# A diffusion trunk layer on eight cores: attention masks added on TensorE, normalizing passes on GpSimd, and a new order of projections and attention

## The reference

```
h    = modulate(layer_norm(x), shift, scale)             # adaLN from SiLU(c) @ w_ada
q, k, v, u, vb, ga, gb = split(h @ w_in)
ya   = attention(rope(q), rope(k), v)                    # band of +-128 tokens, plus 256 context keys,
                                                         # plus a sink logit; 8 query, 2 key heads
yb   = gelu(u) * (W_s @ layer_norm(gelu(vb)) + b_s)      # per chunk of 128 tokens
mix  = (sigmoid(ga) * (ya @ w_a) + sigmoid(gb) * (yb @ w_b)) @ w_out
xm   = layer_norm(alpha * x + gate1 * mix)
out  = layer_norm(alpha * xm + gate2 * swiglu(modulate(layer_norm(xm))))
```

## Time and profile before

| | us |
|---|---|
| median of 3 runs | 969.98 (969.21 to 974.94) |
| the profiled execution | 974.86 |
| its slowest core (core 6), first to last instruction | 973.1 |
| its quickest core (core 5) | 966.4 |
| PE busy on core 6 | 890.9 (92%) |
| DVE, ACT, POOL busy | 622.9, 317.7, 284.6 |

### The profile page before, as it was taken

One profiled execution on the slowest core, in us unless ns is written; L12 is line 12 of the kernel. 1 busy time (PEld: TensorE's weight loads), 2 busy tenths in 40 slices (PEclk: granted clock), 3 DMA queues, 4 the chain that ended last, 5 costly groups with the idle time before them and its releaser, 6 DMA issues.

```text
span 973.1 us, 15750 instructions; the slowest of 8 cores (966.4 to 973.1 us)
## 1 busy us (share of the span) xinstructions
PE 890.9 (92%) x5495; PEld 446.2 (46%) x5589; DVE 622.9 (64%) x1131; ACT 317.7 (33%) x494; POOL 284.6 (29%) x231
## 2 busy tenths in 40 slices
PE   1389688898999999999999999999999999999995
PEld 1235444344554444444444544444444444444673
DVE  4337686857655666766687476556656674666787
ACT  1436775546867243334435200111111001011110
POOL 6024263555554233324312540202202021111111
PEclk9999898979999999999999999999999999999999
DMA  8997622339963500026321480303213020111112
GB/s 203 202 187 190 174 87 66 88 46 161 164 95 81 174 1 1 1 88 100 114 47 44 173 192 25 87 1 87 36 52 87 0 44 1 44 44 57 52 66 87
DMA packets 30380, 83.91 MB, mean 86 GB/s; under 512 B 2912, under 2 KB 3168, under 8 KB 28640
## 3 DMA queue, kind: packets, MB, share of 16 engines
q0 software_dynamic: 18064, 34.54, 22.9%
q1 hardware_dynamic: 12240, 48.37, 14.2%
HBM read 109.05 MB, written 8.39 MB: 121 GB/s over the span
## 4 chain that ended last, share of the span: by engine, by line
PE 84%; DMA 6%; DVE 4%; issue 3%; ACT 2%; POOL 1%; DVEq 0%; POOLq 0%; SPq 0%; ACTq 0%
PE psum L1178 31%; PE psum L1204 15%; PE psum L1016 11%; PE psum L1033 6%; PE psum L1067 6%; DMA arena<-wqk 4%; PE psum L673 3%; PE psum L729 3%; PE psum L900 2%; PE psum L936 2%; PE psum L760 2%; DMA arena<-ctxb 1%; DVE arena L495 1%; PE psum L1102 1%; DVE arena L974 1%
## 5 line engine op out<-in xcount | busy, mean ns | idle before, releaser
L1178 PE MATMUL psum<-arena 128*128 128x512 bf16 (+1 forms) x1515 | 314.5, 361 | 1.1
L1178 PEld LDWEIGHTS psum<-arena 128*128 128x128 bf16 x1536 | 150.2, 98 | 154.5
L1184 ACT ACTIVATE arena<-psum 128x512 f32<-128x512 f32 (+1 forms) x96 | 53.9, 562 | 380.4 <-PE psum L1178 380.4
L1204 PE MATMUL psum<-arena 128*128 128x512 bf16 x681 | 161.0, 379 | 1.9 <-DVE arena L1187 0.7
L508 POOL TENSOR_TENSOR arena<-arena 128x1 f32<-128x1 f32 (+1 forms) x74 | 70.9, 958 | 287.2 <-DVE arena L506 272.0
L1218 DVE TENSOR_TENSOR arena<-arena,psum 128x512 f32<-128x512 f32 x224 | 140.5, 679 | 18.8 <-PE psum L1204 18.6
L1187 DVE TENSOR_TENSOR arena<-psum,arena 128x512 bf16<-128x512 f32 (+1 forms) x96 | 62.0, 646 | 131.2 <-PE psum L1178 127.8
L1016 PE MATMUL psum<-arena 128*128 128x512 bf16 x498 | 115.7, 379 | 1.4 <-issue 1.0
L495 DVE BATCH_NORM_STATS2 arena<-arena 128x6 f32<-128x512 f32 x152 | 99.7, 685 | 14.5 <-DMA arena<-xh 3.8
L1204 PEld LDWEIGHTS psum<-arena 128*128 128x128 bf16 x704 | 68.6, 98 | 82.7 <-issue 2.6
L906 ACT ACTIVATE arena<-psum 128x1024 bf16<-128x1024 f32 (+1 forms) x100 | 80.7, 852 | 23.2 <-PE psum L900 22.1
(11 more groups left out here) (95 smaller groups left out, 883.2 us busy)
## 6 DMA issues: line engine op xcount, KB each, us to landing
arena<-xh SPq DMA_DIRECT2D x34, 512.0 KB, 7.7
arena<-wada POOLq DMA_DIRECT2D x24, 512.0 KB, 18.0
arena<-wff POOLq DMA_DIRECT2D x11, 1024.0 KB, 9.2
arena<-wff SPq DMA_DIRECT2D x11, 1024.0 KB, 7.0
out<-arena SPq DMA_DIRECT2D x15, 512.0 KB, 2.6
arena<-wc POOLq DMA_DIRECT2D x8, 768.0 KB, 20.0
arena<-wout SPq DMA_DIRECT2D x8, 512.0 KB, 4.4
arena<-rope SPq DMA_DIRECT2D x4, 512.0 KB, 11.5
```

Source lines behind the costliest of these rows:

```text
L1178: ins = e.matmul(bank(ps)[:, 0:n], lhsT=w1v[r][:, k, lo:lo + 128], rhs=h2(k), start=(k == 0), stop=(k == 7))
L1184: s = P.op('act', prio - 150, act_cost(n), lambda e: e.activation(out=sgv(), in_=bank(pg)[:, 0:n], func=AF.Silu), after=[a], takes=[sg], g ...
L1204: ins = e.matmul(bank(ps), lhsT=actv[(r, fi, t)], rhs=w2v[r][:, fi, h * 512:(h + 1) * 512], start=(n == 0), stop=(n == 2 * len(rounds) - 1))
```

## The change

- **Masks.** For tiles 0 to 3 the product on POOL (line 915) goes. In its place a matrix `shut` (0 where a key counts, about -1e30 where not) is made once on DVE, and one more matmul per score block adds it through the identity to the scores in PSUM before the exponential: 4 tiles x 2 blocks x 2 key heads = 16 matmuls of 128x512. Tiles 4 to 15 keep the product.
- **Norm passes.** Groups 2 and 3 normalize their tiles on DVE and POOL in turn instead of all on ACT, the group `hal` on DVE and ACT instead of all on ACT. In `proj_v`, odd tiles do the scaling on POOL (`ZPOOL`), straight from mean and rstd, in place of line 525 on DVE and line 774 on ACT.
- **Loads.** The table `rope 0` waits for piece 5 of `wada`, and with it SP's queue. Group 2's x waits for `wu1` instead of `wu3`. Group 3's first two x tiles get two buffers of their own. The gate pieces 8 to 11 of `wada` wait for the second x tile of group 3 (`ld_x3[1]`) instead of `wvvb`.
- **Order.** The planner's `LAG` of POOL goes from 0.12 to 1.2, some durations rise a little, and nearly every priority of the projections, the spatial mixing and the attention is another number.

```diff
-    LAG = {'pe': 0.24, 'act': 0.10, 'dve': 0.10, 'pool': 0.12, 'sp': 0.1}
+    LAG = {'pe': 0.24, 'act': 0.10, 'dve': 0.10, 'pool': 1.2, 'sp': 0.1}
...
-    rope_load('0', 14, rope_d[0], 512, [])
+    rope_load('0', 14, rope_d[0], 512, [ada_ld[5]])
...
-    norm_group('2', [xh[(9 + i) * 128:(10 + i) * 128, :] for i in range(4)], 29, [ld_wu[3]])
-    norm_group('hal', [xh[0:128, :], xh[17 * 128:18 * 128, :], ctxb[0:128, :], ctxb[128:256, :]], 30, [ld_wu[3]])
+    norm_group('2', [xh[(9 + i) * 128:(10 + i) * 128, :] for i in range(4)], 47.5, [ld_wu[1]], ('dve', 'pool'))
+    norm_group('hal', [xh[0:128, :], xh[17 * 128:18 * 128, :], ctxb[0:128, :], ctxb[128:256, :]], 20.1, [ld_wu[3]], ('dve', 'act'))
...
-            r, st = stat(prio + i, [gvs], 512, [[ge]], EPS)
-            mi = minus(st, prio + i - 20, r)
-            z = P.op('act', prio + i - 20, 0.82, lambda e, st=st, gvs=gvs: e.activation(
-                out=gvs(), in_=gvs(), func=AF.Identity, scale=rstd_of(st), bias=minus_of(st)), after=[mi], gives=[st])
+            r, st = stat(prio + i - -25.3, [gvs], 512, [[ge]], EPS)
             me = 'dve' if i % 2 == 0 else 'pool'
...
+            else:
+                z = P.op('pool', prio + i - 20, 1.0, lambda e, st=st, gvs=gvs: e.tensor_scalar(
+                    out=gvs(), in0=gvs(), scalar1=mean_of(st), scalar2=rstd_of(st), op0=ALU.subtract, op1=ALU.mult),
+                    after=[r], gives=[st])
...
+    shut = V(U0 + 46 * KB, BF16, 4, 128)
+    t_shut = P.op('dve', 58.5, 0.4, lambda e: e.tensor_scalar(
+        out=shut, in0=masks, scalar1=-1.0, scalar2=1e30, op0=ALU.add, op1=ALU.mult), after=[ld_masks, c2])
...
-    norm_group('3', [xh[(13 + i) * 128:(14 + i) * 128, :] for i in range(4)], 64, [ld_wu[1]])
+    ld_x3 = norm_group('3', [xh[(13 + i) * 128:(14 + i) * 128, :] for i in range(4)], 90.5, [ld_wu[1]], ('dve', 'pool'), room=(7, 8, 0, 1, 2, 3))
...
-        ada(8 + n, [(2, 2 * n), (2, 2 * n + 1)], 30 + n, (0, 1, 6, 7), after=[ld_wvvb])
+        ada(8 + n, [(2, 2 * n), (2, 2 * n + 1)], 30 + n, (0, 1), after=[ld_x3[1]])
...
-                                       rhs=qv[x * 64:(x + 1) * 64, :, jt * 128:(jt + 1) * 128], start=True, stop=True)
+                                       rhs=qv[x * 64:(x + 1) * 64, :, jt * 128:(jt + 1) * 128], start=True, stop=mi is None)
+                        if mi is not None:
+                            ins = e.matmul(b[:, i * 512:(i + 1) * 512], lhsT=ident,
+                                           rhs=shut[:, mi:mi + 1, :].to_broadcast([128, 4, 128]), start=False, stop=True)
...
-            attend(j, 62.0 + 4 * j, (6, 7), (4, 5), (0, 1, 2, 3, 4, 7, 8, 9, 10))
+            attend(j, 48.8 + 4 * j, (6, 7), (4, 5), (0, 1, 2, 3, 4, 7, 8, 9, 10))
```

More of the change, by code:

```diff
@@ L421, in build_nc @@
     o_a4 = [o_m, o_m + 4 * KB, o_mg, o_mg + 4 * KB] + [L['qg'] + 16 * KB + 4 * KB * i for i in range(4)]
-    o_xr = [o_wo + 4 * KB * i for i in range(4)] + [L['qg'] + 8 * KB, L['qg'] + 12 * KB, L['vn'] + 4 * KB]
+    o_xr = [o_wo + 4 * KB * i for i in range(4)] + [L['qg'] + 8 * KB, L['qg'] + 12 * KB, L['vn'] + 4 * KB,
+                                               L['qg'] + 24 * KB, L['qg'] + 28 * KB]
     o_xnb = [o_xn, o_xn + 2 * KB, L['vn'] + 12 * KB, L['vn'] + 14 * KB]
@@ L619, in norm_group @@
     def norm_group(name, srcs, prio, after, engs=('act', 'act'), room=(0, 1, 2, 3)):
+        lds = []
         for i in (0, 2):
-            norm_pair(name, i, srcs[i:i + 2], prio + 0.1 * i, engs, after, room)
+            lds += norm_pair(name, i, srcs[i:i + 2], prio + 0.1 * i, engs, after, room)
         for c2 in range(4):
@@ L635, in put @@
                         g = int(name)
-                        t_h[(g, c)] = P.op(eng, prio + 0.6, cost, lambda e, ci=ci, c=c, eng=eng, g=g: modulate_out(
+                        t_h[(g, c)] = P.op(eng, prio + 2.2, cost, lambda e, ci=ci, c=c, eng=eng, g=g: modulate_out(
                             e, eng, hT[:, c, g * 512:(g + 1) * 512], bankb(ps)[:, ci * 512:(ci + 1) * 512], 1, 0, c, 0),
@@ L655, in build_nc @@
     ld_masks = load('pool', 22, 256, masks.rearrange('p a b -> p (a b)'), masks_d, 'masks')
+    ZPOOL = 1
+    MASKPE = 4
     PU = (0, 1, 2, 3)
@@ L804, in fgl @@
         return ins
-    m1 = P.op('pe', 58, 0.7, fgl, after=[c1, c2, ld_wst], takes=[pg], gives=[gh])
+    m1 = P.op('pe', 58, 0.7, fgl, after=[c1, c2, ld_wst, ld_bsbc], takes=[pg], gives=[gh])
     t_bs = P.op('dve', 58, 0.69, lambda e: e.tensor_tensor(out=bsbc, in0=bank(pg), in1=bsbc, op=ALU.add),
@@ L892, in attend @@
             ptv = lambda pt=pt: V(o_pt[sid(pt)], BF16, 8, 128)
+            mi = None
+            if kd == 'w' and s != 1:
+                mi = (0 if j == 0 else 1) if s == 0 else (3 if j == NT - 1 else 2)
             ex = []
@@ L911, in attend @@
             exps.append(mm)
-            if kd == 'w' and s != 1:
-                mi = (0 if j == 0 else 1) if s == 0 else (3 if j == NT - 1 else 2)
+            if mi is not None and j < MASKPE:
+                shut_done.append(mm)
+            elif mi is not None:
                 me = 'dve' if s == 2 and j >= 4 else 'pool'
-                ex = P.op(me, prio + n * 0.1, 1.0 if me == 'dve' else 2.1, lambda e, ptv=ptv, mi=mi: e.tensor_tensor(
+                ex = P.op(me, prio + n * 0.1, 1.1 if me == 'dve' else 2.2, lambda e, ptv=ptv, mi=mi: e.tensor_tensor(
                     out=ptv(), in0=ptv(), in1=masks[:, mi:mi + 1, :].to_broadcast([128, 8, 128]), op=ALU.mult),
@@ L968, in fg @@
             return ins
-        gm = P.op('pe', prio + 0.9, 0.3, fg, after=[t_vn[j], ld_wst], takes=[gb])
+        gm = P.op('pe', prio + 9.5, 0.3, fg, after=[t_vn[j], ld_wst], takes=[gb])
         sb = slot('sbt', 0, 1)
         sbv = lambda: V(L['sbt'] + 2 * KB * sid(sb), F32, 512)
-        a = P.op('dve', prio + 0.9, 0.69, lambda e: e.tensor_tensor(out=sbv(), in0=bank(gb), in1=bsbc, op=ALU.add),
+        a = P.op('dve', prio + -16.2, 0.69, lambda e: e.tensor_tensor(out=sbv(), in0=bank(gb), in1=bsbc, op=ALU.add),
                  after=[gm, t_bs], takes=[sb], gives=[gb])
-        t_yb[j] = P.op('dve', prio + 0.9, 0.8, lambda e: e.tensor_tensor(
+        t_yb[j] = P.op('dve', prio + 17.7, 0.98, lambda e: e.tensor_tensor(
             out=gv[:, :, jt * 128:(jt + 1) * 128], in0=sbv().rearrange('p (a b) -> p a b', a=4),
```

67 lines of the change are left out of this document (36 added, 31 removed).

## The result

The changed kernel takes **957.86 us** (median of 4 runs), the kernel before 972.46 us (4 runs) on the same chip: ratio 0.9841, 95% interval 0.9812 to 0.9871, so 1.3 to 1.9% less. The forecast was 958 us.

A forecast was written before the change was run, and what follows sets the result against it. PE was taken as the bound (busy 92% of the span), with room only before the gates. Gains of 6, 4.5 and 5 us less 3.5 for mask matmuls gave -12 us, hence a median of 958 us, range 947 to 971.

The forecast's parts named there:

- the three gains: Before the gates: 6 us in the first projections, 4.5 in attention tiles 0 and 1, 5 in tiles 2 and 3.
- the start: Up to the first projection: reordered loads of rotation tables and weights change nothing, 0 with 2 us either way.
- sign of being wrong: Forecast is wrong if the first projection starts after 54 us or the clock falls in a stretch where it was full.
- First stretch: Projections up to the first score, 52.28 to 127.75 us: relieving ACT shortens PE's waits, 6 us of 11.6 gained.
- Second: Attention tiles 0 and 1, to 159.86 us: without POOL masks, waits and slow clock shrink, 4.5 of 9.8 us gained.
- Fourth: Attention tiles 2 and 3, 179.08 to 205.99 us: without POOL masks a stall goes, 5 us gained.
- The masks' 3.5 us: Tiles 0 to 3: 16 added mask matmuls on PE at 0.216 us each cost 3.5 us, with nothing hiding them.
- the POOL passes: 4 norm passes and 8 scalings moved to POOL take 17 us there, covered during the projections.
- the mask's stall of line 974: Tiles 2 and 3: POOL instructions hold DVE's line 974 for 4.30 us (0.68 alone); PE then stands 2.81 us.
- Rival 1: POOL's moved work blocks DVE through their shared port lock at 80 to 160 us: 967 us, chance 0.22.
- Rival 2: POOL's queue stands 11 us at the first gate piece, waiting for group 3's second x tile: 980 us, chance 0.10.
- Rival 3: Every wait and the slow clock of the first three rooms before the gates vanish: 946 us, chance 0.15.

The follow-up runs named there:

- passes_act_lists_kept: The changed kernel with its instruction lists kept, only POOL's 4 norm passes and 8 scalings moved back to ACT: 959.03 us, 0.9837 of the kernel before.
- after_again: The changed kernel unaltered, run again as the reference on another chip: 958.75 us, 0.9834 of the kernel before.
- after_third: The changed kernel unaltered, run once more as the reference for a later comparison: 960.28 us, 0.9841 of the kernel before.

## Why the prediction was right

**Bound and sum.** The gain lies where it was looked for, before the gates. The sum of the three gains was 15.5 us; what went is 15.5 us by the estimate above: A 4.0, B 7.3, C 1.3, D 3.7, and 0.7 lost again in E. Of the 2.6 us by which the measured 14.6 (972.46 less 957.86) exceed the forecast's 12, the start is 1.6. Work that moved behind the gates is no gain, since the rest is 1.0 us longer, and 1 us stays unaccounted for. The forecast's gain is thus a fifth too small, and that the time came within 0.2 us of 958 is luck: the kernel before measured 972.46 here and 969.98 when the forecast was made. The signs of being right hold: first score at 119.07 (under 122), no POOL product of 128x1024 before tile 4, no DVE instruction over 2 us before 200 us (longest 1.98), the clock at 1.00 in both attention stretches, first projection at 50.0. The first gate matmul starts at 208.0 on the profiled core, 6 us before the forecast's 214. One sign of being wrong appeared too. The clock in E was 1.00 on seven cores of the kernel before, and it is 0.91 to 0.93 on seven of the changed one. E is no longer for it (19.0 against 19.2 us), because less work stands in it; by the estimate above this is the 0.7 us.

**Sizes that were off.** First stretch: 6 us taken, 4.0 of waiting gone (and 5.6 of work moved out, which the prediction had not looked for). Second: 4.5 taken, 7.3. Fourth: 5 taken, 3.7. They make up for each other, so the total is better than its terms. The masks' 3.5 us came out (3.5 by stretch, 4.2 in the time), but not as priced: "0.216 us each" and "nothing hides it" both failed, with 0.9 us in B, where half was hidden, and 2.6 in D, where each matmul cost 0.32.

**The step that failed: the POOL passes.** Taken at 17 us between 6.6 and 18.9; measured 34.3. The upper bound came from two-input instructions of the same width (2.17 us for 1024), and the one-input pass is nearly twice as slow (4.02 us). It did no harm, since `passes_act_lists_kept` shows the time doesn't depend on where they run.

**The causes that failed.** The first stretch was argued from ACT's relief. Of that, the part that POOL took is worth nothing (0.4 us in the time, 959.03 us, and A no longer than cores differ); for the part that DVE took, and for the smaller waits, no run tells, so what shortened A beyond the moved work stays open. The fourth stretch was argued from the mask's stall of line 974. With the changed kernel's lists and the masks back on POOL, D is 20.2 us, as short as without any masks (20.1), although line 995, which is 974's, still runs for 2.27 us: the lists cured it, and the mask matmuls cost D 2.5 us there. Only in B is the mask's place the cause: 6.0 us, in which the price of the mask matmuls is already paid, since that run has none.

**Rivals.** Rival 1: half seen. DVE's gain (L787) has 1.09 us instead of the 0.68 of a single one, the longest 1.78 (at 158.47 us, beside a POOL instruction of 1.27) and 1.75 (at 99.41, beside one of 1.74), but no PE wait before the gates ends with one. Behind them PE waits 0.5 us for such a gain and 0.7 for one on POOL on this core, 1.2 and 0.7 at most on others. Line 974 itself (994 now) fell to 0.89 us from 1.23 on average. Rival 2: POOL was idle for 0.24 us ahead of its first gate piece (100.86), not 11. Rival 3: PE's excess in A stayed at 7.9 us, so not all went.

## What to carry to other kernels

Where a planner or a table sets the order, an experiment that changes a part and plans anew tests the order too; freeze the lists and edit one instruction. What a part is worth depends on the order around it: the same mask matmuls were worth nothing in the old lists and 4.8 us in the new ones, where they gain 6.0 in one stretch and lose 2.5 in the other (small differences elsewhere are the rest). Look at the placing stretch by stretch, and price an operation on an engine from a row of that very form and with the same neighbours.

## What the runs showed of the hardware

POOL's one-input TENSOR_SCALAR with two operations took 4.02 us for 128x1024 (f32 to bf16) and 2.07 us or more for 128x512, against 2.12 us for a two-input product of 128x1024 in bf16 and 1.27 for a sum of 128x512. DVE does the former in 0.88.

Two score matmuls of 64 rows, one behind the other, started within 0.01 us of each other (161.55 above). With a matmul of 128 rows between them, each of the four started 0.32 us after the last, though matmuls of 128x512 with 128 rows that follow one another take 0.216.

The spread of A between cores with one and the same list comes from waits and from the clock. In `after_again` two cores wait for the same POOL pass, core 4 for 1.56 us until 89.54, core 6 for 2.63 us until 91.11. These are 4.5 us of TensorE, about the first of them behind core 6's wait:

```profile
91.00:95.50 4.50, 4.50 (x44) 1.00 0.96 334
```

```profile
91.00:95.50 4.50, 4.21 (x28) 0.62 0.59 194
```

Core 4 stays at 2.4 GHz; core 6 runs most of the stretch at 1.2 GHz, so 0.38 x 4.5 = 1.7 us are lost behind the wait of 2.6. (The counts, 44 and 28, are of different work.) Over the whole of A core 4 idles 7.3 us at a clock of 0.98 and core 6 9.1 us at 0.92, and A is 62.3 us against 67.5. Such a wait does not always cost the clock: core 3 of `after_third` waits 3.31 us for the pass, and its clock over A is 1.00.
